# Up-projections of two gated networks as seven half-block products on one Trainium2 core

## The reference

```python
def dwconv3(x, w):
    xp = jnp.pad(x, ((0, 0), (1, 1), (0, 0)))
    return xp[:, :-2] * w[0] + xp[:, 1:-1] * w[1] + xp[:, 2:] * w[2]

def conv_ffn(a, w_up, conv_w, w_down):
    g, u = jnp.split(dwconv3(a @ w_up, conv_w), 2, axis=-1)
    return (jax.nn.silu(g) * u) @ w_down
```

## Time and profile before

| | |
|---|---|
| Median of three executions | 2996.56 us (2992.07 to 2998.43) |
| Profiled execution, its own time | 2993.15 us |
| Its span, first to last instruction | 2991.4 us |
| PE, PEld, DVE busy | 97%, 86%, 60% of the span |
| ACT, POOL busy | 43%, 16% |
| DMA | 95 GB/s in the mean |

### The profile page before, as it was taken

The page is one execution under the profiler, slowest core; times in us unless marked ns, Lnnn a source line. Parts: engine busy times, 40 slices in busy tenths (PEclk is TensorE's granted clock), DMA queues, the critical chain, the costliest instruction groups (busy, mean ns, idle before and its releaser), DMA issues.

```text
span 2991.4 us, 46812 instructions
## 1 busy us (share of the span) xinstructions
PE 2913.9 (97%) x19658; PEld 2583.3 (86%) x19658; DVE 1797.0 (60%) x2666; ACT 1300.3 (43%) x2153; POOL 483.1 (16%) x405
## 2 busy tenths in 40 slices
PE   6998999999999999999999999999999999999999
PEld 6997887899999999999999977667888878788887
DVE  7776664579597453547949757655535543465453
ACT  4575664344243455644424445654323332343231
POOL 0002221123032000002303313001202111121020
PEclk9998997999999999999999999999999999999999
DMA  2210000245554321025545520102232222223232
GB/s 103 89 53 36 2 2 6 75 156 183 170 170 164 113 88 36 1 79 183 176 164 189 188 99 29 43 17 83 94 97 88 97 90 93 91 85 101 90 97 86
DMA packets 79554, 284.34 MB, mean 95 GB/s; under 512 B 8528, under 2 KB 9296, under 8 KB 78576
## 3 DMA queue, kind: packets, MB, share of 16 engines
q1 hardware_dynamic: 79344, 281.35, 28.1%
HBM read 274.96 MB, written 6.36 MB: 94 GB/s over the span
## 4 chain that ended last, share of the span: by engine, by line
PE 93%; DVE 4%; ACT 2%; issue 1%; POOL 1%; DMA 0%; SPq 0%; DVEq 0%; ACTq 0%
PE psum L348 67%; PE psum L2733 2%; PE psum L1893 2%; PE psum L912 2%; PE psum L2104 2%; PE psum L2086 1%; PE psum L2077 1%; PE psum L1269 1%; PE psum L848 1%; PE psum L539 1%; PE psum L1319 1%; PE psum L1286 1%; PE psum L2430 1%; PE psum L2727 1%; PE psum L2721 1%
## 5 line engine op out<-in xcount | busy, mean ns | idle before, releaser
L303 DVE TENSOR_TENSOR wlo<-wraw,whi 128x1024 fp32r<-128x1024 f32 (+2 forms) x398 | 507.7, 1297 | 614.7 <-ACT whi L296 605.8
L296 ACT CAST whi<-wraw 128x1024 fp32r<-128x1024 f32 (+2 forms) x398 | 396.3, 1021 | 495.2 <-PE psum L348 460.6
L431 DVE CUSTOM_DVE_ANT_0 araw<-araw,cond 128x1024 f32<-128x1024 f32 x112 | 181.1, 1654 | 0.0
L348 PE MATMUL psum<-f0xh,whi 128*128 128x264 f32 x704 | 143.1, 285 | 0.0
L348 PE MATMUL psum<-f0xh,wlo 128*128 128x264 f32 x704 | 143.0, 285 | 0.0
L348 PE MATMUL psum<-f0xl,whi 128*128 128x264 f32 x704 | 142.4, 284 | 0.0
L348 PE MATMUL psum<-f1xh,whi 128*128 128x258 f32 x704 | 141.9, 283 | 0.0
L348 PE MATMUL psum<-f1xh,wlo 128*128 128x258 f32 x704 | 141.9, 283 | 0.0
L348 PE MATMUL psum<-f1xl,whi 128*128 128x258 f32 x704 | 141.4, 282 | 0.0
L348 PE MATMUL psum<-f2xh,whi 128*128 128x512 f32 x352 | 139.1, 395 | 1.0 <-DVE f2xl L592 1.0
L348 PE MATMUL psum<-f3xh,whi 128*128 128x512 f32 x352 | 139.1, 395 | 1.0 <-DVE f3xl L592 1.0
(11 more groups left out here) (515 smaller groups left out, 8193.9 us busy)
## 6 DMA issues: line engine op xcount, KB each, us to landing
wraw<-d_w SPq DMA_DIRECT2D x357, 512.0 KB, 3.4
araw<-d_ada SPq DMA_DIRECT2D x112, 512.0 KB, 3.3
wraw<-d_w SPq DMA_DIRECT2D x32, 384.0 KB, 3.6
hn<-d_h SPq DMA_DIRECT2D x4, 528.0 KB, 7.9
hres<-d_h SPq DMA_DIRECT2D x1, 2112.0 KB, 8.2
spill<-hres SPq DMA_DIRECT2D x1, 2112.0 KB, 7.4
hres<-spill SPq DMA_DIRECT2D x1, 2112.0 KB, 8.5
cond<-d_cond SPq DMA_DIRECT2D x2, 1024.0 KB, 4.8
```

The source lines that it names most:

```text
L296: e.copy(whi[0:rows, n % NH, 0:kt * cols], wraw[0:rows, n % NR, 0:kt * cols]).then_inc(*w_hi.up(n))
L303: e.tensor_tensor(wlo[0:rows, n % NH, 0:kt * cols], wraw[0:rows, n % NR, 0:kt * cols], whi[0:rows, n % NH, 0:kt * cols].bitcast(F32), ALU. ...
L348: ins = e.matmul(psum[0:bw, b0 + nb * len(sl) + si, 0:ln], l_ if z == 2 else h_, (xp.lo if z == 1 else xp.hi)[:, k, o:o + ln], start=k == ...
L431: e.tensor_tensor_reduce(out=w, in0=w, in1=self.c[:, col, :], scale=1.0, scalar=0.0, op0=ALU.mult, op1=ALU.add, accum_out=ada[:, ly, blk, ...
```

## The change

In f2 and f3 the pairs 2 to 21 (twenty in each network, called quads below) take the four quarters of the problem (two halves of the input channels, two halves of the tokens, gate and value) and make seven products in place of eight, in the Winograd form of Strassen's rule. A product has 4 k blocks x 3 parts = 12 matmuls of 256 columns. The parts of it:

- **TensorE**: `seven_pe` does 84 matmuls of 256 columns per quad where there were 48 of 512. Products 2, 4 and 6 go on in a bank into which another engine has just copied or out of which it has just read.
- **Weights**: per quad seven factors of 128 x 512, each with its own cast (ACT) and its own rest (DVE, now scalar_tensor_tensor). Four of the seven are sums or differences that POOL makes first from the raw chunks (`w_sum_pool`), three of them in place. The rings hold six half slots, and an item is split when the item six before it has been used. A raw slot is free for the next load after these sums and rests.
- **State**: the normalisation keeps all eight temporary tiles. POOL makes 16 sums and differences of 128 x 256 from them (`turn_first`, `turn_sums`), and ACT and DVE split these (`turn_act`, `turn_dve`, four rounds each). Pairs 0 and 1 stay as they were, and the first quad waits for the last of these.
- **After the products**: ACT copies two banks on into other banks and evicts three parts of 256 columns. DVE adds two (`tensor_tensor` from PSUM and SBUF). The first tap of the convolution moves from DVE to ACT. The work on a quad's hidden block is laid into the next quad.
- All other stages keep their instructions. Chunks that are not in quads are split as before.

```diff
+SEVEN = ("f2", "f3",)
+PLAIN = 2
...
+ITEMS, PLACE, PREV, FREED = weight_items(6)
+AHEAD = dict(zip(ITEMS[1:], ITEMS))
+SUM_OF = {1: 0, 2: 1, 4: 2, 6: 3}
...
         def w_dma(e, n):
             _, _, _, kt, rows, cols = PLAN[n]
-            if n >= NR:
-                e.wait_ge(*w_lo.at(n - NR))
+            m = n - NR
+            if m >= 0:
+                tag, j, k, *_ = PLAN[m]
+                if not by_seven(tag, j):
+                    e.wait_ge(*w_lo.at(m))
+                elif k == 0:
+                    e.wait_ge(*w_lo.at(m, 4))
+                    e.wait_ge(*w_sum.at(m, 3))
+                else:
+                    e.wait_ge(*w_lo.at(m - 1, 6))
...
+                e.copy(w_place(whi, n, i), factor_of(n, i)).then_inc(*w_hi.up(n, i))
...
+                e.scalar_tensor_tensor(out=w_place(wlo, n, i), in0=factor_of(n, i), scalar=1.0,
+                                       in1=w_place(whi, n, i).bitcast(F32), op0=ALU.mult,
+                                       op1=ALU.subtract).then_inc(*w_lo.up(n, i))
...
+        def w_sum_pool(e, n, s):
+
+            if s == 0:
...
+                e.tensor_tensor(pair_sum(n), quarter(n, 0), quarter(n, 1), ALU.subtract).then_inc(*w_sum.up(n, 0))
+            elif s == 1:
+                raw_here(e, n + 1)
+                e.wait_ge(*w_sum.at(n, 0))
+                e.tensor_tensor(quarter(n, 1), quarter(n + 1, 1), pair_sum(n), ALU.subtract).then_inc(*w_sum.up(n, 1))
+            elif s == 2:
+                e.wait_ge(*w_sum.at(n, 1))
+                e.wait_ge(*w_lo.at(n, 0))
+                e.tensor_tensor(quarter(n, 0), quarter(n, 1), quarter(n, 0), ALU.add).then_inc(*w_sum.up(n, 2))
+            else:
+                e.wait_ge(*w_lo.at(n, 3))
+                e.tensor_tensor(quarter(n + 1, 0), quarter(n + 1, 0), quarter(n, 1), ALU.subtract).then_inc(*w_sum.up(n, 3))
...
+        def seven_pe(e, n, b, X, ready):
...
+            steps = [(b, plain(0, first)), (b + 3, turned(2)), (b + 1, turned(3)), (b, plain(4, first)), (b + 2, turned(0)),
+                     (b + 1, turned(1)), (b + 2, plain(4, second))]
+            for i, (bank, operand) in enumerate(steps):
+                e.wait_ge(*w_lo.at(n, i))
+                ready(e, i)
+                wh, wl = w_place(whi, n, i), w_place(wlo, n, i)
+                for k in range(4):
+                    for z in range(3):
+                        ins = e.matmul(psum[:, bank, 0:half], (wl if z == 2 else wh)[:, k, :], operand(z, k),
+                                       start=i < 2 and k == 0 and z == 0, stop=k == 3 and z == 2, skip_group_check=True)
+                ins.then_inc(*w_used.up(n, i))
...
+        def quad_pe(e, F, p):
...
+                elif i == 2:
+                    e.wait_ge(*f_ev.at(f, p, 0))
+                elif i == 4:
+                    e.wait_ge(*f_ev.at(f, p, 1))
+                elif i == 6:
+                    e.wait_ge(*f_ad.at(f, p, 0))
...
+            def quad(p, behind):
+
+                n, b = quad_chunk(f, p), quad_bank(p)
+                w_freed(e, w_split_dve, *AHEAD[(n, 0)])
+                w_freed(e, w_split_dve, n, 0)
+                if behind:
+                    tap(p - 1, 0, 1)
+                w_freed(e, w_split_dve, n, 1)
+                if behind:
+                    tap(p - 1, 0, 2)
+                w_freed(e, w_split_dve, n, 2)
+                if behind:
+                    tap(p - 1, 1, 1)
+                w_freed(e, w_split_dve, n, 3)
+                if behind:
+                    tap(p - 1, 1, 2)
+                e.wait_ge(*f_ev.at(f, p, 7))
+                e.wait_ge(*w_used.at(n, 4))
+                e.tensor_tensor(up_slot(F, 2 * p + 1, 1), psum[:, b + 2, 0:half_], F.p7[:, p % 2, :],
+                                ALU.add).then_inc(*f_ad.up(f, p, 0))
+                w_freed(e, w_split_dve, n, 4)
+                e.wait_ge(*w_used.at(n, 5))
+                e.tensor_tensor(up_slot(F, 2 * p + 1, 0), psum[:, b + 1, 0:half_], F.p7[:, p % 2, :],
+                                ALU.add).then_inc(*f_ad.up(f, p, 1))
+                w_freed(e, w_split_dve, n, 5)
...
+                    if more_:
+                        weights(p + 1, (0, 1, 2))
+                    if p > 11 * half:
+                        hidden(p - 1)
+                    if more_:
+                        weights(p + 1, (3,))
+                    if p > 11 * half:
+                        rest(p - 1)
...
-            ffn_pe(e, F2, lambda e: e.wait_ge(*res.at("wino", 5)))
+            ffn7_pe(e, F2, lambda e: e.wait_ge(*res.at("wino", 5)))
```

More of the change, by code:

```diff
@@ L168, with by_seven, weight_items @@
 NCH = len(PLAN)
+SEVEN = ("f2", "f3",)
+PLAIN = 2
+def by_seven(tag, j):
+    if isinstance(tag, tuple):
+        return tag[0] in SEVEN and tag[1] == "up" and 11 * tag[2] + j >= PLAIN
+    return tag == "scin" and "sc" in SEVEN and j >= PLAIN
+def weight_items(halves):
+    items, place, prev, freed, last, pos = [], {}, {}, {}, {}, 0
+    for n, (tag, j, k, *_) in enumerate(PLAN):
+        seven = by_seven(tag, j)
+        for key in ([(n, i) for i in range(7)] if k == 0 else []) if seven else [(n,)]:
+            wide = 1 if seven else 2
+            pos += pos % wide
+            place[key] = pos % halves
+            users = [last[h % halves] for h in range(pos, pos + wide) if h % halves in last]
+            if users:
+                prev[key] = max(users)
+                freed.setdefault(prev[key], []).append(key)
+            for h in range(pos, pos + wide):
+                last[h % halves] = key
+            pos += wide
+            items.append(key)
+    return items, place, prev, freed
+ITEMS, PLACE, PREV, FREED = weight_items(6)
+AHEAD = dict(zip(ITEMS[1:], ITEMS))
+SUM_OF = {1: 0, 2: 1, 4: 2, 6: 3}
 class Sig:
@@ L306, in w_view, with w_freed @@
+        def w_freed(e, split, *key):
+            for item in FREED.get(key, ()):
+                split(e, *item)
         def w_view(n):
             _, _, _, kt, rows, cols = PLAN[n]
[L308 removed]
+            f = lambda t: t[0:rows, PLACE[(n,)] // 2, 0:kt * cols].rearrange("p (k c) -> p k c", k=kt)
             return f(whi), f(wlo), cols
@@ L549, in keep_warm @@
             for _ in range(11):
-                e.matmul(psum[:, bank, 0:512], whi[:, n % NH, 0:128], whi[:, n % NH, 0:512], start=True, stop=True)
+                e.matmul(psum[:, bank, 0:512], whi[:, PLACE[(n,)] // 2, 0:128], whi[:, PLACE[(n,)] // 2, 0:512], start=True,
+                         stop=True)
         NORMS = ["f0", "f1", "cx", "l0", "f2", "sc", "f3"]
+        NORM_TILES = {t: 8 if t in SEVEN else 3 for t in NORMS}
         n_t = sig("n_t", [(t, k) for t in NORMS[2:] for k in range(8)])
@@ L1642, in __init__ @@
                 self.freed = []
-                for half in range(2):
+                for half in range(2 * (f not in SEVEN)):
                     self.freed += [f_u.at(f, 22 * half + 2 * j + 1) for j in range(11)]
@@ new lines, in ffn7_pe, with room @@
+        def ffn7_pe(e, F, start):
+            f, ntok = F.f, F.ntok
+            start(e)
+            rms_pe(e, f, ntok, F.sq, 0)
+            keep_warm(e, (f, "up", 0), 4)
+            lin_pe(e, (f, "up", 0), F.x, PLAIN, ntok, lambda e, k: e.wait_ge(*norm_lo(f, k)), lambda e, j: None)
+            for half in range(2):
+                for p in range(11 * half if half else PLAIN, 11 * half + 11):
+                    quad_pe(e, F, p)
+                def room(e, j):
+                    p = 11 * half + 9 + j // 2
+                    e.wait_ge(*f_ev.at(f, p, 2 + j % 2))
+                    e.wait_ge(*f_ad.at(f, p, 1))
+                lin_pe(e, (f, "dn", half), F.hid, 4, ntok, lambda e, k: e.wait_ge(*f_lo.at(f, 11 * half + k)), room, kt=11,
+                       set0=2 * half, block6=f + "b" if half and f + "b" in LAST.values() else None)
```

358 lines of the change are left out of this document (322 added, 36 removed).

## The result

The changed kernel takes 3117.28 us in the median of four runs (3112.41 to 3123.3), beside 2997.49 us for the kernel before: a ratio of 1.0396, 95% interval 1.0374 to 1.0417. Forecast were 3086 us with a range of 3015 to 3165. The profiled execution spans 3121.5 us at a mean granted clock of 0.964 (before: 2991.4 us, 0.987).

A forecast was written before the change was run, and what follows sets the result against it. PE bounds the kernel before; in the changed quads, turns of DVE and POOL on SBUF would. 2993 + 74 for quads + 16 for network starts = 3083 us profiled, 3086 as median; range 3015 to 3165.

The forecast's parts named there:

- The turns of DVE and POOL: In quads, DVE instructions with two SBUF inputs alternate with POOL's: 0.55 us held by DVE, 1.14 by POOL.
- Two of the signs I had named: In the profile after: rests and taps at means of 1.0 us and more, POOL's 512-column instructions at 1.5 and more.
- The terms of that 13.8: Full quad: DVE's 8.1 us plus six POOL instructions at 1.03 give upper bound 14.3; lower 12.9; taken 13.8.
- The first quad of a network: First quad in each half: no taps or hidden block behind it, 9.5 us of turns, so PE's 9.8 us.
- the whole start ahead of that quad: Each network's start, normalisation through pairs 0 and 1: 8 us more, 16 in all, bounds 0 and 25.
- the last of the halves: Last quad of each half of a network: no sums ahead, so 10.2 us.
- The forecast of the mechanism alone: Whole kernel by DVE and POOL's turns and start cost, without the clock: 3041 to 3111 us.
- PE's term: PE's part of a quad: 84 matmuls of 256 columns at 0.117 us, 9.81 us against 11.19 for a pair.
- PE as the bound: Rival: no turns taken in quads, PE stays the bound, kernel at 2940 to 2960 us; chance 0.12.
- In between: Rival: half of the turns hidden under waits, a quad at 11 to 12.5 us, kernel 2975 to 3025; chance 0.05.
- The clock: Rival: PE's pauses in full quads lower its clock, 1.8 us each, 58 us in all, 3144 us; chance 0.17.
- quads wholly at the low level: Aside in the clock rival: 84 matmuls at 0.22 us, 18.5 us a quad, kernel 3320 us; 0.03 for over 3165.

The follow-up runs named there:

- run 3: Changed kernel with POOL's four weight sums per quad, from the third quad on, cut to 8 of 512 elements: 2989.97 us; or made full-width memsets: 2984.37 us.
- Run 4: Changed kernel with the four weight sums of each quad moved from POOL to DVE: 3046.01 us, ratio 1.0161 to the kernel before.
- run 2: Changed kernel with 20 unused matmuls on PE ahead of its wait for product 6, to keep the clock high: 3114.9 us, ratio 1.0394 to the kernel before.
- the best version found: Changed kernel with quads only at pairs 5, 7, ... 21 and reordered ACT, DVE and POOL work: 2991.22 us, ratio 0.9978 to the kernel before.

## Why the prediction was right, and where it was off

**The bound.** Right. The turns of DVE and POOL that the earlier trace rows showed elsewhere came with the change: rests at 1.31 us, POOL's L394 at 1.70 and L2222 at 1.66 us. A full quad takes 13.88 us (forecast 13.8, 12.9 to 14.3), and runs 3 and 4 show that it is POOL's reading that lengthens it. Two of the signs I had named did not come. Taps stay at 0.82 us in the mean, where I had written 1.0 and more for rests and taps: of 69 taps counted in f2's quads POOL lengthens 5. And not all of POOL's instructions became long. L2218 keeps 1.30 us and L405 1.33; in the quad shown they start ahead of the rest that they delay (L2218 at 2349.44, the rest at 2349.55). f2's stretch is 429 us where I had 415, and PE is busy for 87% of it and not 80%: it stands still for 2.5 us a quad and not 4, because its slowed matmuls fill the rest (22.9 us busy in two quads, at full clock 19.8).

**The terms of that 13.8.** Two errors that cancel. Rests cost 0.60 and adds 0.33 us apart, not 0.66 and 0.41 (DVE alone 7.5 us, not 8.1), and a POOL instruction takes 1.08 us from DVE, not 1.03. That the 13.8 is so close is partly luck. Run 4, in which the two terms do not cancel, would have come to 12.8 by my terms and came to 12.1.

**The first quad of a network, the step that failed.** I priced it at PE's 9.8 us, with no taps behind it; it takes 21.2 us, 11.4 more, in both networks. The chain of waits of the changed kernel at that place:

```profile
2083.83 1.15 DVE f2Tl L1975
2084.98 1.76 DVE f2Tl L1980 x2
...
2097.79 0.79 DVE f2Tl L1980 x2
2098.58 1.22 DVE wlo L383 x2
2099.87 2.27 POOL wraw L405
2102.16 0.63 ACT whi L370
2102.81 1.10 DVE wlo L383
```

The error is to have summed the quad's own work as if it could be done ahead, and to have left out the taps of pair 1, which do stand behind a network's first quad. DVE comes to it straight from the turned state at 2098.6 us, when PE is already at product 1, after a wait of 3.7 us. Eight rests (five of this quad, three of the next) and pair 1's four taps lie between there and product 6, and the fifth of these rests waits for POOL's last sum and the cast behind it, as the chain shows. PE waits another 4.4 us for the add. The remaining 3.3 us are the low clock after the two pauses (0.81 over products 1 to 5, 0.50 over product 6). I had put 8 us for the whole start ahead of that quad, and it is 4.8. PE waited 3.7 us for the turned state, not over 12. The same mistake, smaller: the first quad of the second half 11.1 in place of 9.8, the last of the halves 12.5 and 11.8 in place of 10.2. That DVE enters them late from the full quads was not tested for these.

**The sum.** Against 2 x 45 us forecast stand 119.8, 30 more: first quads 2 x 11.4 and 2 x 1.3, last quads 2 x 3.9, full quads 2 x 1.3, start 2 x -3.2, together +29. The forecast of the mechanism alone ended at 3111 us, below the 3117 measured. The time lies in the stated range because I had widened that to 3165 for the clock, which was not the cause; that part is luck. PE's term was a little off too: 84 matmuls take 9.90 us in these quads, not 9.81.

**The rivals.** PE as the bound: refuted, at 13.88 us a quad; run 3 shows what would have made it true. In between, at 11 to 12.5 us a quad: refuted by the same number. The clock: its sign is there only in part, 0.88 in two quads and 0.94 over f2, where I had set "well under 0.9", and run 2 takes it away and the time stays. The slowed products do delay DVE's casts, but the add does not come later for it; only in the first quad of a network does the clock lie on the path. The aside in that rival on quads wholly at the low level does not add up: 18.5 us a quad would be about 3237 us for the 32 full quads and 3305 for all 40, not 3320. The rule of the Trainium skill (SBUF — State Buffer, section SBUF: two separate sides), by which whichever of the two engines starts first keeps the shared path for the whole instruction, gave 16.1 us a quad. Measured are 13.88, and 1.08 us of POOL's 1.30 are taken. The 16.1 was worked out from latencies, which overlap from one instruction to the next, so it is more than the rule would give by start distances.

## What to carry to other kernels

Before work is given to POOL to relieve DVE, price it on DVE's side: here each POOL instruction with two SBUF operands took 1.08 us from DVE, which does the same work itself in 0.60. A sum of work per period says little of the first period: follow the engine's queue from the last thing that it does before it. And a saving of one eighth of PE's products (1.29 us in 11.19) needs every other engine's chain to be shorter than the period; in this kernel it is about the same length, and the best version found gains 0.2%.

## What was not expected of the hardware

- A POOL memset of 128 x 512 (0.53 us) beside DVE's two-operand instructions costs them nothing (0.69 and 0.74 us), while a two-operand instruction on tiles of the same size costs them 1.08 us. That it is the reading is the simplest account; other POOL forms with one operand were not tried.
- A granted clock of 0.91 against 1.00 over 56 us made hardly a difference to the time (55.98 and 55.83 us) where DVE bounds.
- The kernel with quads from pair 5 ran between 2984.71 and 3000.93 us in one series, more than its gain; only the interval over 12 runs tells it from the kernel before. The granted clock goes with it: 0.988 in the fastest of them, 0.980 in the slowest. What moves it was not looked into.
